# Reordering the start of the attention steps in the compressed-key layers of a four-layer hybrid transformer

## The chip, the cores and the metric

The kernel runs on one core of one Trainium2 chip. The metric is device time in microseconds of one execution, as a median over executions. Lower is better.

## The reference

Four layers over 512 tokens of width 1024 (16 heads of 64). Each layer is a mixer and a gated convolutional feed-forward part, with RMS norms around both. The mixers are, in order: nsa (compressed keys, selected keys, local window), stick-breaking, sliding window with sinks, and nsa again. The change concerns the two nsa layers. Cut to what matters:

```python
q, k_cmp, v_cmp, k_sel, v_sel, k_win, v_win, g_logit = split(h @ w_in)
ck, cv = compress(k_cmp, 0), compress(v_cmp, 1)        # 31 compressed keys for each of 4 groups
for each block i of 128 queries, each group g, each head r of the group:
    p_cmp = masked_softmax(q @ ck.T * scale - slope * dist_c);   o_cmp = p_cmp @ cv
    # the 16 best blocks of 64 keys are asked for, and there are only 8: all are selected
    p_s   = masked_softmax(q @ k_sel.T * scale - slope * dist);  o_sel = p_s @ v_sel
    p_w   = masked_softmax(q @ k_win.T * scale - slope * dist);  o_win = p_w @ v_win
    out   = g0 * o_cmp + g1 * o_sel + g2 * o_win
return out @ w_out
```

All is float32. masked_softmax divides by max(sum, 1e-30); that maximum is the "floor" below.

## The kernel before

**Weights and panels.** Weights stream from HBM in units of 128 x 1024 through a ring of four (L239). ScalarE rounds a unit to its high part (L260, `split_hi`), VectorE forms the low part (L266, `split_lo`), and TensorE multiplies high by high, low by high and high by low (L304 to L306, and L917 to L919 in key and value panels). A panel is four units into four of the eight PSUM banks. Panel S holds selected keys and values, panel W the window ("local") ones.

**Between the panels.** While TensorE works on S and W, VectorE makes the softmax of the compressed scores (`lowered`, `weighted`, `turned`, L1835 to L1851), takes the selected keys out of PSUM into the scratch `ktmp` (`dve_k`, L1002), and forms their low halves in `kl` (`dve_k_low`, L967 and L974), which raises `k_ready`. ScalarE copies values (`act_v`, L1007) and the keys' high halves (`act_k`, L957). `ktmp` lies at the address `u2_at`, and so does `qs`, the queries of the current group, split in two: ScalarE writes the high half (L1347), VectorE the low half (L1407), four of each for the four heads of a group. Since both share the address, the first queries wait for `k_ready`.

**Steps.** Behind the panels come 64 steps (`STEPS`): 4 groups x 2 kinds of keys (selected, then local) x 2 pairs of heads x 4 query blocks, the largest first (`step_of`: i = 3, 2, 1, 0, with i + 1 key blocks). For each step t and both heads of the pair:

1. TensorE `scores(t)` (L1285, L1286), issued four steps ahead. The first two (`ahead`) are issued inside W's last unit, the third behind it and behind `pe.wait_ge(evac_v, v_after[W + 1])`, the evacuation of the local keys.
2. VectorE `biased(t)` (L1419): bias and row minimum.
3. ScalarE `exps(t)` (L1355): exponential and sum.
4. VectorE `floor(t)` (L1450) and `inverse(t)` (L1455) of the sums.
5. GpSimd `weighted(t)` (L1501): times inverse and gate. It raises `nd_done`.
6. TensorE `transposes(t)` (L1298) into two PSUM banks.
7. ScalarE `copy(t)` of the first bank (L1363) and VectorE `copy(t)` of the second (L1429). For i = 3 and 2 each head has a bank. For i = 1 both heads lie in the first bank (ScalarE's), for i = 0 both lie in the second (VectorE's).
8. TensorE `values(t)` (L1319).

The order on each engine is written out by hand: `pe_steps`, `act_steps`, `dve_steps`, `pool_steps`. TensorE runs transposes(t), scores(t + 4), values(t - 1) in each step. VectorE's local keys are `window_keys` (L1002 again, into `kts`); their low halves (`window_low`, L1437 and L1440) are spread over steps 1 to 8. The output of two heads is `output` on ScalarE (L1374) and `low` on VectorE (L1445), the latter raising `o_ready`. Then follows the output projection (`pe_out`).

VectorE's order at the head of the steps:

```python
queries(0, 0)
queries(0, 1)
biased(0)
biased(1)
window_keys()
queries(0, 2)
queries(0, 3)
for t in range(2):
    floor(t)
    inverse(t)
biased(2)
biased(3)
```

Of the kernel before, what the change touches and what calls it, by code (L numbers as in the profile page):

```python
# [6 lines left out]
F32 = mybir.dt.float32  # L7
# [5 lines left out]
P = 128  # L13
D = 1024
T = 512
# [88 lines left out]
def hybrid_layers(nc, ins, out, kinds=KIND):  # L104
# [7 lines left out]
    with ExitStack() as ctx:  # L112
# [660 lines left out]
        for c, start in ((0, t_start), (1, o_at)):  # L773
            xcf.append(Space(start, start + 8 * K)(f"xcf{c}", [P, 16, G, N_CMP], F32))
            xcl.append(Space(start, start + 8 * K)(f"xcl{c}", [P, 16, G, N_CMP], F32R))
            xch.append(Space(start + 8 * K, start + 16 * K)(f"xch{c}", [P, 16, G, N_CMP], F32R))
        ktmp = Space(u2_at, u2_at + 4 * K)("ktmp", [P, 2, T], F32)
        hs = Space(o_at, o_at + 8 * K)
# [482 lines left out]
        def act_copies(t):  # L1261
            return 3 * (t // 4) + (1, 2, 3, 3)[t % 4]
# [4 lines left out]
        def pe_steps(pe, l, last_unit):  # L1267
# [20 lines left out]
            def transposes(t):  # L1288

                it, b, p, i = step_of(t)  # L1290
                pe.wait_ge(nd_done, 2 * (B + t) + 2)
                if t:
                    pe.wait_ge(nca_done, C3 + act_copies(t - 1))
                    pe.wait_ge(ncd_done, C3 + dve_copies(t - 1))
                for a in range(2):
                    x, at_ = turned_at(t, a)
                    for j in range(i + 1):
                        mm = nc.tensor.transpose(psum[:, half_of(l, 4 + x), at_ + j * P:at_ + (j + 1) * P],  # L1298
                                                 raw_scores(t, a)[:, j * P:(j + 1) * P], ident[:])
                    mm.then_inc(nt_done, 1)  # L1300
# [36 lines left out]
            values(STEPS - 1)  # L1337

        def act_steps(act, l, window_values):
            k = nsa_before[l]  # L1340
            B = STEPS * k

            def queries(it, r):
                s_ = slice(64 * (r % 2), 64 * (r % 2) + 64)
                if it:
                    act.wait_ge(nz_done, 2 * (B + 16 * (it - 1) + 8 + 4 * (r // 2) + 4))
                nc.scalar.activation(qs[s_, r, :], qt[s_, 2 * it + r // 2, :], ACT.Copy, scale=1.0 / slope(R * it + r)).then_inc(qh_done, 1)  # L1347

# [26 lines left out]

            act.wait_ge(k_ready, kr_before[l] + 2)
            for r in range(R):
                queries(0, r)
            exps(0)
# [3 lines left out]
            for t in range(STEPS):  # L1383
                it, x = t // 16, t % 16
                if step_of(t)[3]:
                    copy(t)
                if t + 3 < STEPS:
                    exps(t + 3)
                if it == 0 and x in (1, 3, 5, 7):
                    window_twin(x // 2)  # L1390
                if it + 1 < G and x in (8, 9, 12, 13):
                    queries(it + 1, (8, 9, 12, 13).index(x))
                if x == 13:
                    output(2 * it)
                if x == 1 and it:
                    output(2 * it - 1)
            output(DC - 1)

        def dve_steps(dve, ch, l, window_keys):
            k = nsa_before[l]  # L1400
            B = STEPS * k

            def queries(it, r):
                a = r % 2
                s_, d_ = slice(64 * a, 64 * a + 64), slice(64 * (1 - a), 64 * (1 - a) + 64)
                dve.wait_ge(qh_done, heads_before[l] + R * it + r + 1)
                nc.vector.scalar_tensor_tensor(qs[d_, r, :], qt[s_, 2 * it + r // 2, :], 1.0 / slope(R * it + r),  # L1407
                                               qs[s_, r, :].bitcast(F32), ALU.mult, ALU.subtract).then_inc(qs_ready, 1)

# [46 lines left out]

            mark = [0]
            queries(0, 0)
            queries(0, 1)
            biased(0)  # L1460
            biased(1)
            window_keys()
            queries(0, 2)
            queries(0, 3)
            for t in range(2):
                floor(t)
                inverse(t)
            biased(2)
            biased(3)
            for t in range(STEPS):  # L1470
                it, x = t // 16, t % 16
                if t + 2 < STEPS:
                    floor(t + 2)
                if step_of(t)[3] != 1:
                    copy(t)
                if t + 2 < STEPS:
                    inverse(t + 2)
                if t + 4 < STEPS:
                    biased(t + 4)
                if it == 0 and 1 <= x <= 8:  # L1480
                    window_low(x - 1)
                if it + 1 < G and x in (9, 10, 13, 14):
                    queries(it + 1, (9, 10, 13, 14).index(x))
                if x == 14:
                    low(2 * it)
                if x == 2 and it:
                    low(2 * it - 1)
# [217 lines left out]
        def act_nsa(act, ch, l):  # L1705
# [25 lines left out]
            def exps(half):  # L1731
                act.wait_ge(ca_done, 2 * k + half + 1)
                v = sp_[:, 2 * half:2 * half + 2, :]
                nc.scalar.activation(v, v, ACT.Exp, scale=-1.0).then_inc(ce_done, 1)

            exps(0)
            act_v(act, ch, 0, p0 + 4, u0 + 24)
# [7 lines left out]
        def dve_nsa(dve, ch, l):  # L1745
# [106 lines left out]

            lowered(0)
            dve_k(dve, ch, l, 0, p0 + 4, u0 + 24, 2)
            dve.wait_ge(kt_done, kc_before[l] + 2)
            dve.sem_inc(evac_v, 1)
            split_lo(dve, u0 + 24 + AHEAD)
            lowered(1)
# [552 lines left out]
```

## Time and profile before

| what | value |
|---|---|
| median of 3 runs | 2602.22 us (2601.59 to 2604.24) |
| the profiled execution | 2604.24 us |
| its span in the trace | 2602.5 us |
| mean granted TensorE clock | 0.994 |
| TensorE busy | 2525.7 us, 97% |
| VectorE / ScalarE / GpSimd busy | 62% / 45% / 18% |

The span runs from the first to the last instruction of the program. "Idle before" a group is the time its engine stood still just ahead of it, and the arrow names what released it. PEclk is the share of TensorE's full clock that was granted. Times in the trace are in us from the span's start. The first nsa layer's steps run from about 151 to 303, the fourth layer's from about 2023 to 2174.

### The profile page before, as it was taken

The page shows a single profiled execution, that of the slowest core. Times are in us where ns is not written, and L with a number is a line of the kernel's source. Part 1 is how long each engine was busy: PE and PEld are TensorE (multiplying, and loading weights), DVE is VectorE, ACT ScalarE, POOL GpSimd, SP SyncE. Part 2 cuts the span into 40 slices and gives each one's busy share as a digit, 9 for nine tenths or more (in the row PEclk, how much of TensorE's full clock was granted, in tenths as well). Part 3 has the DMA queues.
Part 4 walks back from the last instruction along what each step waited for, and adds up shares of the span by engine and source line. Part 5 has one row for each costly group of instructions (what it writes and reads, how often), then busy time and mean ns, then how long its engine had stood idle before and what let it go on. Part 6 is the DMA issues. An engine that isn't in the chain of part 4 may idle for free.

```text
span 2602.5 us, 38223 instructions
## 1 busy us (share of the span) xinstructions
PE 2525.7 (97%) x13336; PEld 2076.2 (80%) x13336; DVE 1623.6 (62%) x2773; ACT 1171.2 (45%) x2007; POOL 473.1 (18%) x514
## 2 busy tenths in 40 slices
PE   8999999999999999999999999999999899999997
PEld 6977778888878677888878878888879777788886
DVE  6588567664263847667256677663385884766733
ACT  4367554443232844444235554442343674544421
POOL 2035321110010612111010021110010452211100
PEclk9999999999999999999999999999999999999999
DMA  4410123333233022333321123333333001233231
GB/s 159 140 33 2 33 79 100 97 97 97 75 109 97 17 65 92 96 96 94 103 79 61 42 81 100 96 96 99 97 106 108 17 2 51 88 97 97 89 105 49
DMA packets 61909, 210.91 MB, mean 81 GB/s; under 512 B 8528, under 2 KB 10320, under 8 KB 61776
## 3 DMA queue, kind: packets, MB, share of 16 engines
q1 hardware_dynamic: 61776, 209.13, 25.6%
q8 instruction: 84, 1.38, 0.2%
q14 instruction: 49, 0.40, 0.0%
HBM read 207.01 MB, written 2.10 MB: 80 GB/s over the span
## 4 chain that ended last, share of the span: by engine, by line
PE 86%; DVE 10%; ACT 2%; issue 1%; POOL 1%; DMA 0%; DVEq 0%; SPq 0%; POOLq 0%; ACTq 0%
PE psum L304 21%; PE psum L306 21%; PE psum L305 21%; PE psum L1298 3%; PE psum L1319 2%; PE psum L917 2%; PE psum L918 2%; PE psum L919 2%; DVE xl L477 2%; DVE h L494 2%; PE psum L1286 1%; PE psum L1285 1%; PE psum L338 1%; DVE dh L493 1%; PE psum L332 1%
## 5 line engine op out<-in xcount | busy, mean ns | idle before, releaser
L304 PE MATMUL psum<-xh,w_hi 128*128 128x512 f32 x1712 | 666.7, 389 | 0.2 <-DVE w_lo L266 0.2
L305 PE MATMUL psum<-xh,w_lo 128*128 128x512 f32 x1712 | 666.1, 389 | 0.0
L306 PE MATMUL psum<-xl,w_hi 128*128 128x512 f32 x1712 | 666.1, 389 | 0.0
L266 DVE TENSOR_TENSOR w_lo<-w_raw,w_hi 128x1024 fp32r<-128x1024 f32 x226 | 279.9, 1250 | 531.4 <-ACT w_hi L260 529.3
L260 ACT ACTIVATE w_hi<-w_raw 128x1024 fp32r<-128x1024 f32 x226 | 236.0, 1057 | 591.7 <-PE psum L306 465.1
L306 PEld LDWEIGHTS psum<-xl,w_hi 128*128 128x128 f32 x1712 | 321.3, 188 | 66.9
L304 PEld LDWEIGHTS psum<-xh,w_hi 128*128 128x128 f32 x1712 | 321.3, 188 | 66.8 <-issue 0.6
L305 PEld LDWEIGHTS psum<-xh,w_lo 128*128 128x128 f32 x1712 | 321.4, 188 | 66.5
L698 DVE TENSOR_TENSOR w_lo<-w_raw,w_hi 128x1024 fp32r<-128x1024 f32 x160 | 209.3, 1308 | 253.8 <-ACT w_hi L694 253.8
L669 POOL TENSOR_TENSOR cv<-cv 128x512 f32<-128x512 f32 x88 | 133.9, 1521 | 792.9 <-ACT cv L623 785.4
L694 ACT ACTIVATE w_hi<-w_raw 128x1024 fp32r<-128x1024 f32 x160 | 168.4, 1053 | 234.8 <-PE psum L306 234.8
L305 PE MATMUL psum<-ah,w_lo 128*128 (+1 forms) x704 | 273.9, 389 | 0.0
L304 PE MATMUL psum<-ah,w_hi 128*128 (+1 forms) x704 | 273.9, 389 | 0.0
L306 PE MATMUL psum<-al,w_hi 128*128 (+1 forms) x704 | 273.9, 389 | 0.0
L618 ACT ACTIVATE cv<-xo,conv_b,conv_w 128x512 f32<-128x512 f32 x176 | 129.2, 805 | 95.4 <-DVE xo L642 95.4
L651 DVE SCALAR_TENSOR_TENSOR cv<-xo,conv_w,cv 128x512 f32<-128x512 f32 x176 | 169.6, 1003 | 0.6 <-DVE xo L642 0.6
L305 PEld LDWEIGHTS psum<-ah,w_lo 128*128 128x128 f32 x704 | 132.1, 188 | 27.5
L304 PEld LDWEIGHTS psum<-ah,w_hi 128*128 128x128 f32 x704 | 132.1, 188 | 27.5
L306 PEld LDWEIGHTS psum<-al,w_hi 128*128 128x128 f32 x704 | 132.1, 188 | 27.3
L623 ACT ACTIVATE cv<-cv 128x512 f32<-128x512 f32 x88 | 55.0, 625 | 173.6 <-DVE cv L656 173.6
L1501 POOL TENSOR_SCALAR scores<-scores,rsums,gat 128x384 f32<-128x384 f32 (+1 forms) x128 | 98.2, 777 | 190.0 <-DVE rsums L1455 190.0
L332 PE MATMUL psum<-xh,w_hi 128*128 128x512 f32 (+1 forms) x284 | 105.8, 379 | 23.5 <-ACT xh L553 12.9
(217 smaller groups left out, 4049.0 us busy)
## 6 DMA issues: line engine op xcount, KB each, us to landing
w_raw<-w_up SPq DMA_DIRECT2D x176, 512.0 KB, 3.6
w_raw<-w_down SPq DMA_DIRECT2D x88, 512.0 KB, 3.6
w_raw<-nsa_in SPq DMA_DIRECT2D x56, 512.0 KB, 4.1
w_raw<-sb_in SPq DMA_DIRECT2D x24, 512.0 KB, 3.6
w_raw<-nsa_out SPq DMA_DIRECT2D x16, 512.0 KB, 3.6
w_raw<-swa_in SPq DMA_DIRECT2D x10, 512.0 KB, 3.6
w_raw<-sb_out SPq DMA_DIRECT2D x8, 512.0 KB, 3.7
w_raw<-swa_out SPq DMA_DIRECT2D x8, 512.0 KB, 3.6
```

Of the source, the lines that this page charges most:

```text
L260: nc.scalar.activation(w_hi[:, u % RING, :], w_raw[:, u % RING, :], ACT.Copy).then_inc(hi_done, 1)
L266: nc.vector.tensor_tensor(w_lo[:, u % RING, :], w_raw[:, u % RING, :], w_hi[:, u % RING, :].bitcast(F32), ALU.subtract).then_inc(split_don ...
L304: nc.tensor.matmul(bank(p, o), wh[:, k, o, :], xhi(k), start=(first and k == 0), stop=False)
L305: nc.tensor.matmul(bank(p, o), wl[:, k, o, :], xhi(k), start=False, stop=False)
L306: mm = nc.tensor.matmul(bank(p, o), wh[:, k, o, :], xlo(k), start=False, stop=(last and k == 1))
L332: nc.tensor.matmul(bank(p, o)[:, lo:hi], wh[:, k, o, :], xh[:, c, lo:hi], start=(c == 0 and lo == 0), stop=False, skip_group_check=True)
L618: nc.scalar.activation(cv[:, o, :], xo[:, o, 2:T + 2], ACT.Identity, bias=conv_b[:, bass.ds(cc, 1)], scale=conv_w[:, 2, bass.ds(cc, 1)]).t ...
L651: marks.append(ch.then(nc.vector.scalar_tensor_tensor(cv[:, o, :], xo[:, o, 1:T + 1], conv_w[:, 1, bass.ds(cc, 1)], cv[:, o, :], ALU.mult, ...
L669: nc.gpsimd.tensor_tensor(cv[:, 2 + a, :], cv[:, a, :], cv[:, 2 + a, :], ALU.mult).then_inc(prod_done, 1)
L694: nc.scalar.activation(w_hi[:, u % RING, :], w_raw[:, u % RING, :], ACT.Copy).then_inc(hi_done, 1)
L698: nc.vector.tensor_tensor(w_lo[:, u % RING, :], w_raw[:, u % RING, :], w_hi[:, u % RING, :].bitcast(F32), ALU.subtract).then_inc(split_don ...
L1501: nc.gpsimd.tensor_scalar(v, v, rsums[:, c:c + 1], gat[:, i, x:x + 1], ALU.mult, ALU.mult).then_inc(nd_done, 1)
```

## The change

Five moves, all in the nsa layers:

- `ktmp` goes to the address `o_at`, so the queries' buffer is free earlier. The queries of group 0 are split ahead of the compressed exponentials on ScalarE, and around the evacuation of the selected keys on VectorE, two ahead and two behind. ScalarE's wait for `k_ready` ahead of them goes. The functions move out as `act_query` and `dve_query`.
- On VectorE the floors and inverses of steps 0 and 1 go ahead of the local keys.
- TensorE's transpositions wait for the bank that they write, ScalarE's or VectorE's, in place of both at the start of a step.
- VectorE's copy for i = 0 goes ahead of the floor.
- `low(2 * it)` goes from the 15th step of a group to the 16th.

```diff
@@ -774,7 +774,7 @@
             xcf.append(Space(start, start + 8 * K)(f"xcf{c}", [P, 16, G, N_CMP], F32))
             xcl.append(Space(start, start + 8 * K)(f"xcl{c}", [P, 16, G, N_CMP], F32R))
             xch.append(Space(start + 8 * K, start + 16 * K)(f"xch{c}", [P, 16, G, N_CMP], F32R))
-        ktmp = Space(u2_at, u2_at + 4 * K)("ktmp", [P, 2, T], F32)
+        ktmp = Space(o_at, o_at + 4 * K)("ktmp", [P, 2, T], F32)
         hs = Space(o_at, o_at + 8 * K)
         hb = hs("hb", [NX, 2, CMP_HID], F32)
         hid = hs("hid", [P, 2, NX], F32)
@@ -1289,11 +1289,12 @@
 
                 it, b, p, i = step_of(t)
                 pe.wait_ge(nd_done, 2 * (B + t) + 2)
-                if t:
-                    pe.wait_ge(nca_done, C3 + act_copies(t - 1))
-                    pe.wait_ge(ncd_done, C3 + dve_copies(t - 1))
                 for a in range(2):
                     x, at_ = turned_at(t, a)
+                    if t and x == 0:
+                        pe.wait_ge(nca_done, C3 + act_copies(t - 1))
+                    elif t:
+                        pe.wait_ge(ncd_done, C3 + dve_copies(t - 1))
                     for j in range(i + 1):
                         mm = nc.tensor.transpose(psum[:, half_of(l, 4 + x), at_ + j * P:at_ + (j + 1) * P],
                                                  raw_scores(t, a)[:, j * P:(j + 1) * P], ident[:])
@@ -1336,15 +1337,24 @@
                     values(t - 1)
             values(STEPS - 1)
 
+        def act_query(act, l, it, r):
+            s_ = slice(64 * (r % 2), 64 * (r % 2) + 64)
+            if it:
+                act.wait_ge(nz_done, 2 * (STEPS * nsa_before[l] + 16 * (it - 1) + 8 + 4 * (r // 2) + 4))
+            else:
+                act.wait_ge(q_done, qn_before[l] + 2)
+            nc.scalar.activation(qs[s_, r, :], qt[s_, 2 * it + r // 2, :], ACT.Copy, scale=1.0 / slope(R * it + r)).then_inc(qh_done, 1)
+
+        def dve_query(dve, l, it, r):
+            a = r % 2
+            s_, d_ = slice(64 * a, 64 * a + 64), slice(64 * (1 - a), 64 * (1 - a) + 64)
+            dve.wait_ge(qh_done, heads_before[l] + R * it + r + 1)
+            nc.vector.scalar_tensor_tensor(qs[d_, r, :], qt[s_, 2 * it + r // 2, :], 1.0 / slope(R * it + r),
+                                           qs[s_, r, :].bitcast(F32), ALU.mult, ALU.subtract).then_inc(qs_ready, 1)
+
         def act_steps(act, l, window_values):
             k = nsa_before[l]
             B = STEPS * k
-
-            def queries(it, r):
-                s_ = slice(64 * (r % 2), 64 * (r % 2) + 64)
-                if it:
-                    act.wait_ge(nz_done, 2 * (B + 16 * (it - 1) + 8 + 4 * (r // 2) + 4))
-                nc.scalar.activation(qs[s_, r, :], qt[s_, 2 * it + r // 2, :], ACT.Copy, scale=1.0 / slope(R * it + r)).then_inc(qh_done, 1)
 
             def exps(t):
                 n = (step_of(t)[3] + 1) * P
@@ -1373,9 +1383,6 @@
                 act.wait_ge(nv_done, B + 16 * (c // 2) + 12 + 4 * (c % 2))
                 nc.scalar.activation(xh[:, c, :], psum[:, half_of(l, 6 + c % 2), :], ACT.Copy).then_inc(oh_done, 1)
 
-            act.wait_ge(k_ready, kr_before[l] + 2)
-            for r in range(R):
-                queries(0, r)
             exps(0)
             exps(1)
             window_values()
@@ -1389,7 +1396,7 @@
                 if it == 0 and x in (1, 3, 5, 7):
                     window_twin(x // 2)
                 if it + 1 < G and x in (8, 9, 12, 13):
-                    queries(it + 1, (8, 9, 12, 13).index(x))
+                    act_query(act, l, it + 1, (8, 9, 12, 13).index(x))
                 if x == 13:
                     output(2 * it)
                 if x == 1 and it:
@@ -1399,13 +1406,6 @@
         def dve_steps(dve, ch, l, window_keys):
             k = nsa_before[l]
             B = STEPS * k
-
-            def queries(it, r):
-                a = r % 2
-                s_, d_ = slice(64 * a, 64 * a + 64), slice(64 * (1 - a), 64 * (1 - a) + 64)
-                dve.wait_ge(qh_done, heads_before[l] + R * it + r + 1)
-                nc.vector.scalar_tensor_tensor(qs[d_, r, :], qt[s_, 2 * it + r // 2, :], 1.0 / slope(R * it + r),
-                                               qs[s_, r, :].bitcast(F32), ALU.mult, ALU.subtract).then_inc(qs_ready, 1)
 
             def biased(t):
 
@@ -1455,23 +1455,22 @@
                 nc.vector.reciprocal(rsums[:, 16 + c:18 + c], rsums[:, 8 + c:10 + c]).then_inc(nw_done, 1)
 
             mark = [0]
-            queries(0, 0)
-            queries(0, 1)
             biased(0)
             biased(1)
-            window_keys()
-            queries(0, 2)
-            queries(0, 3)
             for t in range(2):
                 floor(t)
                 inverse(t)
+            window_keys()
             biased(2)
             biased(3)
             for t in range(STEPS):
                 it, x = t // 16, t % 16
+                i = step_of(t)[3]
+                if i == 0:
+                    copy(t)
                 if t + 2 < STEPS:
                     floor(t + 2)
-                if step_of(t)[3] != 1:
+                if i >= 2:
                     copy(t)
                 if t + 2 < STEPS:
                     inverse(t + 2)
@@ -1480,8 +1479,8 @@
                 if it == 0 and 1 <= x <= 8:
                     window_low(x - 1)
                 if it + 1 < G and x in (9, 10, 13, 14):
-                    queries(it + 1, (9, 10, 13, 14).index(x))
-                if x == 14:
+                    dve_query(dve, l, it + 1, (9, 10, 13, 14).index(x))
+                if x == 15:
                     low(2 * it)
                 if x == 2 and it:
                     low(2 * it - 1)
@@ -1733,6 +1732,8 @@
                 v = sp_[:, 2 * half:2 * half + 2, :]
                 nc.scalar.activation(v, v, ACT.Exp, scale=-1.0).then_inc(ce_done, 1)
 
+            for r in range(R):
+                act_query(act, l, 0, r)
             exps(0)
             act_v(act, ch, 0, p0 + 4, u0 + 24)
             split_hi(act, u0 + 24 + AHEAD)
@@ -1851,9 +1852,13 @@
                 nc.vector.tensor_copy(ct[:, :, i * P:(i + 1) * P], bank(p0 + 5, 2 + i % 2).rearrange("p (g q) -> p g q", q=P)).then_inc(cpt_ready, 1)
 
             lowered(0)
+            dve_query(dve, l, 0, 0)
+            dve_query(dve, l, 0, 1)
             dve_k(dve, ch, l, 0, p0 + 4, u0 + 24, 2)
             dve.wait_ge(kt_done, kc_before[l] + 2)
             dve.sem_inc(evac_v, 1)
+            dve_query(dve, l, 0, 2)
+            dve_query(dve, l, 0, 3)
             split_lo(dve, u0 + 24 + AHEAD)
             lowered(1)
             weighted(0)
```

## Rows read from the trace of the kernel before

**Rows 1.** The page, part 1: busy time, share and instructions of each engine.

```profile
PE 2525.7 (97%) x13336; PEld 2076.2 (80%) x13336; DVE 1623.6 (62%) x2773; ACT 1171.2 (45%) x2007; POOL 473.1 (18%) x514
```

**Rows 2.** TensorE's waits, 120 to 320: us in total, times, longest.

```profile
PE psum L1298 <- DVE pt L1429: 3.9, 7, 1.2
PE psum L1285 <- DVE qs L1407: 2.6, 1, 2.6
PE psum L1298 <- POOL scores L1501: 2.4, 1, 2.4
```

**Rows 3.** TensorE's waits over the whole span.

```profile
PE psum L332 <- ACT xh L553: 12.9, 7, 1.9
...
PE psum L1298 <- DVE pt L1429: 8.1, 15, 1.2
```

**Rows 4.** Timeline of TensorE: start, us, instruction, idle before it, releaser.

```profile
154.07 0.47 PE L1285 MATMUL psum<-kh,qs 128*128 128x512 f32 x1 [2.63 <-DVE qs L1407]
...
160.34 0.38 PE L1285 MATMUL psum<-kh,qs 128*128 128x256 f32 x1
...
163.86 1.09 PE L1298 MATMUL psum<-ident,scores 128*128 128x128 f32 x8 [2.39 <-POOL scores L1501]
```

**Rows 5.** Windows: length, busy time of each engine, PEclk, DMA share, GB/s.

```profile
155.10:158.40 3.30, 3.30 (x10) 2.89 (x9) 2.06 (x8) 2.72 (x8) 0.00 (x0) 0.50 0.08 31
165.30:168.60 3.30, 3.30 (x13) 2.96 (x12) 2.79 (x10) 2.24 (x8) 2.34 (x5) 0.50 0.03 7
...
1882.20:1885.50 3.30, 3.30 (x14) 2.91 (x13) 3.23 (x6) 2.68 (x4) 0.00 (x0) 0.50 0.91 291
```

**Rows 6.** Timeline of VectorE, 126 to 161.

```profile
126.44 1.29 DVE L1002 TENSOR_TENSOR ktmp<-psum,rb 128x512 f32<-128x512 f32 x2 [1.86 <-PE psum L919]
129.34 1.23 DVE L266 TENSOR_TENSOR w_lo<-w_raw,w_hi 128x1024 fp32r<-128x1024 f32 x1 [1.62 <-ACT w_hi L260]
...
150.38 0.86 DVE L974 CAST kl<-kl 64x512 fp32r<-64x512 f32 x2
...
154.81 0.69 DVE L1419 CUSTOM_DVE_ANT_0 scores<-psum,dist 128x512 f32<-128x512 f32 x1 [0.89 <-PE psum L1286]
...
157.13 0.08 DVE L1419 DVE_READ_ACCUMULATOR2_ANT mins<- 128x1 f32 x1
158.94 1.29 DVE L1002 TENSOR_TENSOR kts<-psum,rb 128x512 f32<-128x512 f32 x2 [1.72 <-PE psum L919]
160.38 1.40 DVE L1407 SCALAR_TENSOR_TENSOR qs<-qt,qs 64x512 fp32r<-64x512 f32 x2 [0.15 <-DVE kts L1002]
```

**Rows 7.** Timeline of ScalarE, 119 to 165.

```profile
124.62 1.06 ACT L1734 ACTIVATE scores<-scores 128x1024 f32<-128x1024 f32 x1 [6.28 <-DVE scores L1838]
...
151.26 2.59 ACT L1347 ACTIVATE qs<-qt 64x512 fp32r<-64x512 f32 x4 [1.49 <-DVE kl L974]
155.54 0.72 ACT L1355 ACTIVATE scores<-scores,mins 128x512 f32<-128x512 f32 x1 [1.69 <-DVE mins L1419]
...
158.07 0.19 ACT L1355 ACTIVATION_READ_ACCUMULATOR scores<-scores,mins 128x1 f32 x1
```

**Rows 8.** The chain that ended last, at GpSimd's first products.

```profile
162.29 0.22 POOL scores L1501
...
163.04 0.78 POOL scores L1501
```

**Rows 9.** Timeline of all engines, 189.5 to 192.5: step 12.

```profile
189.90 1.99 POOL L1501 TENSOR_SCALAR scores<-scores,rsums,gat 128x512 f32<-128x512 f32 x2 [1.18 <-DVE rsums L1455]
...
191.28 0.64 DVE L1450 TENSOR_SCALAR rsums<-rsums 128x2 f32<-128x2 f32 x1
...
192.38 0.30 PE L1298 MATMUL psum<-ident,scores 128*128 128x128 f32 x1 [1.18 <-DVE pt L1429]
```

**Rows 10.** Windows of groups 0 and 1, from first transposition to first transposition.

```profile
163.86:201.00 37.14, 35.25 (x305) 27.90 (x305) 33.12 (x118) 29.46 (x85) 24.29 (x36) 0.95 0.01 2
201.00:236.00 35.00, 34.14 (x309) 26.66 (x310) 28.58 (x117) 27.65 (x83) 20.13 (x33) 1.00 0.01 1
```

## The prediction, made before the changed kernel was run

> **What bounds the kernel now.** I read the page first. TensorE is busy for 97% of the span, VectorE for 62%, ScalarE for 45%, GpSimd for 18% [rows 1]. A change that only reorders work can therefore give back only what TensorE stands idle, or what it runs at a low clock. Next I read TensorE's waits for the first compressed-key (nsa) layer alone [rows 2]. Three kinds fall into it: 2.6 us once, for the low halves of the queries (L1407), 2.4 us once, for GpSimd's weighted probabilities (L1501), and 3.9 us in seven pieces, for VectorE's copies of transposed probabilities (L1429). The fourth layer is the same code, and the whole-span row for L1429 has 8.1 us in 15 pieces [rows 3]. I work out one layer and double it.
>
> The timelines show where the two long stalls stand. The first scores begin at 154.07 after 2.63 us, the first transposition at 163.86 after 2.39 us [rows 4]. Each is followed by a stretch at granted clock 0.50 (the 1.2 GHz level): 155.1 to 158.4, and 165.3 to 168.6 [rows 5]. So a stall is paid once as idle time and a second time in half-speed matmuls. Scores and the rest of the panel took 160.34 - 154.07 = 6.27 us [rows 4]. At full rate I estimate 4.7 us: four products of 512 at 0.23, four of 384 at 0.17, half a unit at 1.38 + 1.6, taken from the starts in the stretch at full clock. The cost is 1.6 us. For the second stretch I take 1.5 us, the 3.3 us at half speed less a little waiting inside it.
>
> **The change, part by part, from 151.44 on, in one layer.**
>
> *Queries early.* The scratch of the selected keys leaves the queries' address, so the eight splits can run before the keys are done. On ScalarE four cost 2.59 us and go into a wait of 6.28 us [rows 7]. On VectorE two cost 1.40 us (0.69 each, L1407 at 160.38) and go into the wait of 1.86 us ahead of the keys at 126.44; the other two come behind the keys (1.29 us, to 127.7) and end at 129.1, and the next instruction began at 129.34 [rows 6]. All of it is covered; uncovered it would be 2.8 us on VectorE. The first scores then wait for the lows of the selected keys, whose last cast ends at 150.38 + 0.86 = 151.24 [rows 6]. That is 0.2 us ahead of TensorE's need at 151.44, so they start at 151.4. Gain 2.6 us, and 1.6 us of half clock: the first unit ends at 151.4 + 4.7 = 156.1 in place of 160.34. No DMA is moved; the weights' high halves stand ahead of ScalarE's queries in its order, as before.
>
> *Floors and inverses ahead of the local keys.* VectorE still has a weight split first, to 152.4. The four biased scores took 157.13 + 0.08 - 154.81 = 2.40 us, so they end at 154.8 [rows 6]. ScalarE's exponentials end 3.45 us behind the first biased one (154.81 to 158.26) [rows 6, 7]: 155.85. The second floor needs these, so floors and inverses end at 156.35. Only then come the local keys, 1.29 us [rows 6]: 157.65. In front of its third scores TensorE waits for just that evacuation. It was ready at 156.1 and goes on at 157.75: a new stall of 1.65 us. Two scores of 256 and two of 128 columns take 1.0 us, and transposition 0 starts at 158.8. GpSimd needed 163.82 - 162.29 = 1.53 us for its first two products [rows 8]; they now begin at 155.3, and hide. So 163.86 becomes 158.8: 5.06 us gained (2.6 + 1.6 + 2.4 - 1.65 = 4.95 by parts, the same within rounding). What is queued behind the floors is the evacuation, and all of TensorE waits for it.
>
> Without a long stall the second half-clock stretch goes too: 1.5 us.
>
> *Transposition waits by bank, and the one-block copy ahead of the floor.* Beyond the two stalls I count 4.1 us of small ones in this layer: 3.9 us [rows 2] and 0.2 us of pieces under 0.16 us. At step 12 TensorE waits 1.18 us. VectorE's floor lasts 0.64 us there, where its others take 0.17, and ends at 191.92, just as GpSimd's pair does (189.90 + 1.99 = 191.89); the copy comes behind it [rows 9]. Putting the copy first takes it out from behind the floor, but transposition 12 also needs GpSimd's pair, so only 192.38 - 192.0 = 0.4 us comes back. The other six waits make 3.9 - 1.2 = 2.7 us [rows 2], 0.36 to 0.51 us each. Five stand at steps 16, 28, 32, 44 and 48, where GpSimd's pair ends some 0.1 us ahead of TensorE, so I take all of them: 2.2 us. The sixth, 0.5 us at step 61, is for a copy of three blocks; with waits by bank its first three transpositions go ahead, and 0.35 us comes back. Sum 3.0 us, between 0 and 4.1.
>
> *The low half of the output one step later.* It costs the same 0.69 us and now follows the copy. Its reader in the next group comes two steps later, at about 238, and it ends near 236.3. Nothing.
>
> *What is late next.* In the first group VectorE also splits the local keys. It is busy 33.12 us there, against 28.58 in the next group [rows 10], and its timeline shows no wait from 173 to 193. Group 0 took 37.14 us and would now take about 34.8, so VectorE has hardly any room. Some of what TensorE gains at the beginning comes back at step 12, since VectorE's idle 2.2 us before 173.2 existed only because TensorE was slow. I charge 0.7 us, between 0 and 1.5 us.
>
> Sum for one layer: 2.6 + 1.6 + 2.4 - 1.65 + 1.5 + 3.0 - 0.7 = 8.75 us; for two, 17.5 us. The profiled execution has a span of 2602.5 us within its own 2604.24; the median of the three is 2602.22. 2602.5 - 17.5 = 2585.0 for the span, and 2602.2 - 17.5 = 2584.7 for the time.
>
> **A rule to weigh.** The floor that ends with GpSimd's pair [rows 9] is a row about a shared path. The Trainium skill (SBUF - State Buffer, section "Who interferes with whom") says that a VectorE instruction in a two-port mode and a GpSimd instruction exclude each other for the whole of whichever began first. It speaks against this change in one place: the second floor now comes while GpSimd works on its first products. By the rule it waits up to one product, 0.7 us, and the evacuation and TensorE behind it with it; the sum would be 2584.9 to 2586.1, against 2584.7 with a floor of 0.17 us.
>
> **The rivals.**
>
> *The new stall brings the half clock back.* TensorE has seven idle times of 12.9 / 7 = 1.84 us in the span [rows 3]; behind two of them the clock fell to 0.50, at 1882.2 and at 2223.5, and not behind the other five (the first of the two is in [rows 5]). Behind all four of 2.4 to 2.6 us it fell, behind the two of 1.18 us it did not. A stall of 1.65 us lies below, so a fall is perhaps one in four for each layer, at 1.6 us: 2586.3 with one, 2587.9 with two.
>
> *VectorE becomes the bound of the steps.* If it runs late through all groups, the 3.0 us of small waits stay and the charge doubles: 2 x 3.7 us less, 2592.1. For it speaks the busy time of group 0; against it the 6.4 us that VectorE stands idle in group 1, of 35.0 [rows 10].
>
> *Everything gives way.* No new stall, all small waits gone, no charge: 2 x 3.45 us more, 2577.8. Against it: the evacuation stands behind the second floor in one queue.
>
> *The queries do not let the scores go.* If the four splits delay VectorE's softmax, the lows of the keys come late by the same, and 2.6 + 1.6 us fall away in each layer: 2593.1. The covers above speak against it.
>
> *Slower than before.* The floors wait for ScalarE, and the evacuation of the local keys waits behind them. If that chain were late for another reason, TensorE would stand at this one wait. It would have to stand 1.65 + 8.75 = 10.4 us in each layer before the change loses. The exponentials are four instructions of about 0.7 us, so nothing in the profile makes that so long.
>
> **How the numbers follow.** Forecast, no clock fall or one of them, with its own range 2582 to 2588: 0.58. Two falls, or VectorE somewhat later than charged: 0.12. VectorE the bound: 0.13. Everything gives way: 0.10. Queries without effect: 0.04. Slower: 0.03. The prediction is 2585.0, the worked-out 2584.7 rounded toward the cases above it. The range reaches from 2579 (nearly all gives way) to 2593 (small waits unmended, or both falls with some lateness), and leaves about one in ten on the whole outside. 0.2%, about what a measurement of this kernel can tell from no change, is 5.2 us. All cases but the last lie below 2597; for gains that shrink further than any of these I keep 0.04. Faster 0.93, within 0.2% 0.04, slower 0.03.
>
> **What would show it.** First scores some 0.1 us behind the panel's matmul in place of 2.63. A wait of TensorE for L1002 of 1 to 2 us ahead of the third scores, which is not there now. No wait for L1501 at the first transposition. Both L1347 and L1407 near 118 to 129. Small waits on L1429 under 2 us in a layer. The clock at 1.00 through 151 to 175. The prediction is wrong if the first scores still wait, if the stall at the local keys is over 3 us, or if VectorE shows no idle time in groups 1 to 3 while TensorE waits for it.

## The result, and the profile after

The changed kernel takes 2586.23 us (median of 4 runs, 2583.41 to 2587.39), against 2603.23 us for the kernel before in the same comparison. The ratio is 0.9933, with a 95% interval of 0.9918 to 0.9948. The prediction was 2585.0 in a range of 2579 to 2593. The profiled execution took 2587.39 us, with a span of 2585.6.

The page's first part, to be read against [rows 1]: TensorE is busy 3.7 us less though it does the same matmuls, and the span is 16.9 us shorter, so 13.2 us of idle time went and the rest is clock.

```profile
span 2585.6 us, 38223 instructions
...
PE 2522.0 (98%) x13336; PEld 2073.5 (80%) x13336; DVE 1623.5 (63%) x2773; ACT 1170.1 (45%) x2007; POOL 472.6 (18%) x514
```

TensorE's waits over the whole span (us in total, times, longest). The copies (L1429), 8.1 us in [rows 3], are gone, and so are the queries (2.6 us in each layer, [rows 2]). In their place stands L1285, released by VectorE's queue, 1.6 us in each layer. GpSimd's products (now L1500) hold 1.8 us where they held 4.8. The line with 4.8 is of the kernel before, the others of the changed one:

```profile
PE psum L1298 <- POOL scores L1501: 4.8, 2, 2.4
```

```profile
PE psum L332 <- ACT xh L553: 13.0, 7, 1.9
...
PE psum L1285 <- DVEq L1878: 3.2, 2, 1.6
PE psum L1299 <- POOL scores L1500: 1.8, 2, 1.0
```

TensorE's timeline in the first layer, against [rows 4]. The first scores follow the panel without a wait, the third ones wait 1.61 us, and the first transposition follows at once. The last line is step 12, against [rows 9].

```profile
151.68 0.47 PE L1285 MATMUL psum<-kh,qs 128*128 128x512 f32 x1
...
157.94 0.39 PE L1285 MATMUL psum<-kh,qs 128*128 128x256 f32 x1 [1.61 <-DVEq L1878]
...
158.93 1.85 PE L1299 MATMUL psum<-ident,scores 128*128 128x128 f32 x8
...
187.01 1.09 PE L1299 MATMUL psum<-ident,scores 128*128 128x128 f32 x8 [0.97 <-POOL scores L1500]
```

VectorE's timeline, against [rows 6]. The four early splits (L1352) take what was idle; the weight split behind them starts at 129.69, at once behind its high half (ScalarE's, 128.60 + 1.06 = 129.66). The second floor waits 0.83 us for ScalarE's exponentials, and the local keys (`kts`) come only behind it:

```profile
124.96 1.41 DVE L1352 SCALAR_TENSOR_TENSOR qs<-qt,qs 64x512 fp32r<-64x512 f32 x2
126.79 1.29 DVE L1002 TENSOR_TENSOR ktmp<-psum,rb 128x512 f32<-128x512 f32 x2 [0.42 <-PE psum L919]
128.23 1.40 DVE L1352 SCALAR_TENSOR_TENSOR qs<-qt,qs 64x512 fp32r<-64x512 f32 x2 [0.15 <-DVE ktmp L1002]
129.69 1.23 DVE L266 TENSOR_TENSOR w_lo<-w_raw,w_hi 128x1024 fp32r<-128x1024 f32 x1
...
155.24 0.17 DVE L1455 RECIPROCAL rsums<-rsums 128x2 f32<-128x2 f32 x1
156.23 0.22 DVE L1450 TENSOR_SCALAR rsums<-rsums 128x2 f32<-128x2 f32 x1 [0.83 <-ACT scores L1365]
156.48 0.17 DVE L1455 RECIPROCAL rsums<-rsums 128x2 f32<-128x2 f32 x1
156.56 1.27 DVE L1002 TENSOR_TENSOR kts<-psum,rb 128x512 f32<-128x512 f32 x2
```

Windows of the changed kernel, columns as in [rows 5]. TensorE is busy 1.79 of the 3.4 us around the new stall, and the 3.3 us behind it run at granted clock 0.50:

```profile
155.50:158.90 3.40, 1.79 (x16) 1.59 (x15) 1.98 (x7) 2.27 (x8) 3.33 (x5) 1.00 0.08 34
159.10:162.40 3.30, 3.30 (x13) 2.81 (x12) 2.22 (x11) 2.22 (x9) 0.65 (x2) 0.50 0.03 7
```

Groups 0 and 1, against [rows 10]. Group 0 has 0.97 us of idle time left and group 1 none, at 34.01 us where it took 35.00:

```profile
158.93:195.08 36.15, 35.18 (x306) 27.78 (x305) 33.38 (x121) 29.92 (x86) 22.13 (x34) 0.95 0.01 2
195.08:229.09 34.01, 34.01 (x310) 26.61 (x309) 28.48 (x115) 27.50 (x83) 20.10 (x32) 1.00 0.01 1
```

For all kernels below I measure the same stretches in the trace of each: from the end of the panel's matmul ahead of the first scores to the first transposition ("start"), the four groups of steps, and the sum to the first matmul of the output projection ("layer"). "Low" counts the half-clock stretches inside it. Values are us in the first layer; the value in brackets is the fourth layer's.

| kernel | start | group 0 | group 1 | group 3 | layer | low, 1st (4th) | span |
|---|---|---|---|---|---|---|---|
| before | 12.42 | 37.14 | 34.96 | 32.47 | 151.94 (152.10) | 2 (2) | 2602.5 |
| changed | 7.15 | 36.16 | 34.01 | 32.11 | 143.42 (143.22) | 1 (1) | 2585.6 |
| e1 queries only | 6.67 | 35.51 | 34.95 | 32.47 | 144.57 (144.56) | 0 (0) | 2588.0 |
| e2 keys first | 6.66 | 34.67 | 34.01 | 32.12 | 141.45 (141.43) | 0 (0) | 2582.0 |
| e3 steps only | 12.41 | 35.96 | 34.01 | 32.11 | 148.50 (148.42) | 2 (2) | 2595.2 |
| e4 wait moved, one floor | 5.29 | 35.29 | 34.01 | 32.11 | 140.71 (140.72) | 0 (0) | 2580.2 |
| e5 no bank waits | 7.14 | 36.58 | 34.04 | 32.52 | 144.32 (143.81) | 1 (1) | 2587.1 |
| e6 bank waits only | 12.40 | 34.47 | 34.06 | 32.16 | 147.13 (147.05) | 1 (1) | 2592.9 |
| e7 lows spread | 7.14 | 33.45 | 34.13 | 32.11 | 140.83 (140.86) | 0 (0) | 2579.8 |
| e8 wait moved | 6.25 | 34.71 | 34.02 | 32.11 | 141.10 (141.40) | 0 (0) | 2581.8 |
| e9 changed again | 7.13 | 34.66 | 34.01 | 32.11 | 141.92 (141.92) | 0 (0) | 2582.4 |
| e10 keys first again | 6.66 | 34.67 | 34.01 | 32.11 | 141.45 (141.53) | 0 (0) | 2580.5 |
| e11 combined | 5.30 | 34.89 | 34.14 | 32.11 | 140.48 (140.45) | 0 (0) | 2579.3 |
| e12 combined, old copy | 5.30 | 34.43 | 34.14 | 32.11 | 140.00 (140.04) | 0 (0) | 2579.1 |

The two layers together lost 17.4 us (304.04 to 286.64), against 16.9 for the span; the rest of the program is the same within 0.6 us. Over all kernels the rest lies between 2297.6 and 2299.3 us. Nearly all of that is the time ahead of the steps: the panel's matmul ahead of the first scores ends between 150.5 (e10) and 152.3 (e12). So differences of a microsecond are read from the layers, not from spans or times. The changed kernel and e1 to e12 were timed in four sets, the last three on different chips; the kernel before took 2603.23 us in the first, 2602.41 in that of e1 to e4, 2602.88 (one execution) in that of e5 to e8 and 2602.48 in that of e9 to e12.

### The profile page after: what moved, and what is told of

Same layout as the page of the kernel before. It is cut to its first block, busy times and chain, and to the rows that moved or that the text cites. A ratio compares the mean times of both kernels' runs of the same rounds, so it can differ in the third digit from the quotient of the medians.

```text
span 2585.6 us, 38223 instructions
## 1 busy us (share of the span) xinstructions
PE 2522.0 (98%) x13336; PEld 2073.5 (80%) x13336; DVE 1623.5 (63%) x2773; ACT 1170.1 (45%) x2007; POOL 472.6 (18%) x514
## 4 chain that ended last, share of the span: by engine, by line
PE 88%; DVE 9%; ACT 1%; issue 1%; POOL 1%; DMA 0%; DVEq 0%; SPq 0%; POOLq 0%; ACTq 0%
PE psum L304 21%; PE psum L306 21%; PE psum L305 21%; PE psum L1299 3%; PE psum L1320 3%; PE psum L917 2%; PE psum L919 2%; PE psum L918 2%; DVE xl L477 2%; DVE h L494 2%; PE psum L1286 1%; PE psum L1285 1%; PE psum L338 1%; DVE dh L493 1%; PE psum L332 1%
## 5 line engine op out<-in xcount | busy, mean ns | idle before, releaser
L1500 POOL TENSOR_SCALAR scores<-scores,rsums,gat 128x384 f32<-128x384 f32 (+1 forms) x128 | 98.1, 776 | 170.1 <-DVE rsums L1455 170.1
```

What stands on the lines that cost most here:

```text
L1500: nc.gpsimd.tensor_scalar(v, v, rsums[:, c:c + 1], gat[:, i, x:x + 1], ALU.mult, ALU.mult).then_inc(nd_done, 1)
```

## The experiments

**e1: the early queries alone**, on the kernel before.

```diff
-        ktmp = Space(u2_at, u2_at + 4 * K)("ktmp", [P, 2, T], F32)
+        ktmp = Space(o_at, o_at + 4 * K)("ktmp", [P, 2, T], F32)
...
+            for r in range(R):
+                act_query(act, l, 0, r)
             exps(0)
             act_v(act, ch, 0, p0 + 4, u0 + 24)
```

> The kernel before with the early queries alone (scratch moved, splits moved); local keys ahead of the floors as before, waits and copies as before. My theory: the first scores start at once and the local keys are evacuated while TensorE still works on its unit, so there is no wait at the third scores. The floors then come behind the keys, and the first transposition waits about 1.1 us for GpSimd's products: first transposition 6.7 us behind the first scores, where the changed kernel has 7.2. The small waits of 4.1 us in a layer stay. Span 2 x (2.6 + 1.6 + 1.3 + 0.5) = 12 us below before, 2590.5; up to 3 us more if the shorter stall no longer brings a half-clock stretch. Rival: without the floors ahead the first transposition waits its old 2.4 us, and the span is 2594 or more.

Measured: 2589.23 us (median of 4 runs), ratio 0.9947 (0.9932 to 0.9962), span 2588.0. The first transposition stood 6.78 us behind the first scores. TensorE's waits in the first layer, by L1298: the two long ones of [rows 2] are one of 1.0 us, and the small ones are just as they were.

```profile
PE psum L1298 <- DVE pt L1428: 3.9, 7, 1.2
PE psum L1298 <- POOL scores L1496: 1.0, 1, 1.0
```

What follows: the early queries give 7.4 and 7.5 us a layer by themselves, the larger part of the change, and do not need the floors ahead. 3.2 us of it is clock, two stretches of 1.6. No half-clock stretch was left, which makes 14.5 us of span in place of the 12 I had summed up, as the expectation allowed.

**e2: the local keys ahead of the floors again**, on the changed kernel.

```diff
+            window_keys()
             for t in range(2):
                 floor(t)
                 inverse(t)
-            window_keys()
```

> The changed kernel with the local keys ahead of the two floors again; all else stays. My theory: the wait of 1.61 us at the third scores goes and one of about 1.1 us comes at the first transposition, so each layer is 0.5 us shorter in idle time, and if a stall of 1.1 us brings no half-clock stretch, 1.5 us more: span between 2581.5 and 2584.6 against 2585.6. Rival, that the floors ahead are what the change needs: the first transposition waits 2.4 us as before, and the span is 2587 or more.

Measured: 2583.73 us (median of 4), ratio 0.9926 (0.9911 to 0.9941), span 2582.0. TensorE's timeline: the third scores run at once, and the first transposition waits 0.95 us.

```profile
156.77 0.39 PE L1285 MATMUL psum<-kh,qs 128*128 128x256 f32 x1
...
158.86 1.09 PE L1299 MATMUL psum<-ident,scores 128*128 128x128 f32 x8 [0.95 <-POOL scores L1500]
```

What follows: with the queries early, the floors ahead of the keys lose. The start is 6.66 us without them and 7.15 with them. The rest of the difference is clock and is taken up at e9.

**e3: the three moves inside the steps alone**, on the kernel before: waits by bank, the one-block copy ahead of the floor, `low` at the 16th step.

> The kernel before with the three moves inside the steps alone: waits by bank, one-block copy ahead of the floor, low half one step later. My theory: both long stalls of 2.6 and 2.4 us and both half-clock stretches stay; of the small waits of 4.1 us in a layer some 0.8 us at step 12 are left. Span 6.0 to 6.8 us below before, about 2596. Rival, VectorE as the bound of the steps: less than 2 us below.

Measured: 2594.94 us (median of 6), ratio 0.9971 (0.9959 to 0.9983), span 2595.2. The start is as long as before and both half-clock stretches stayed; a layer is 3.4 to 3.7 us shorter, and the wait at step 12 is 0.81 and 0.86 us. The gain of 7.5 us is a little over the 6.0 to 6.8 that I expected. VectorE is not the bound.

**e4: the evacuation wait at the first transposition, and one floor ahead of the keys**, on the changed kernel.

```diff
                 window(3, begin)
-                pe.wait_ge(evac_v, v_after[W + 1])
...
                 pe.wait_ge(nd_done, 2 * (B + t) + 2)
+                if t == 0:
+                    pe.wait_ge(evac_v, v_after[plan.mix_p[l] + 7])
...
-            for t in range(2):
-                floor(t)
-                inverse(t)
+            floor(0)
+            inverse(0)
             window_keys()
+            floor(1)
+            inverse(1)
```

> The changed kernel with two more moves: TensorE's wait for the evacuation of the local keys goes from the third scores to the first transposition (scores 2 and 3 write other banks), and of the two floors only the first stands ahead of the local keys. My theory: no wait at the third scores; GpSimd's first pair and the evacuation are both done within 0.1 us of the end of scores 3, so no idle time over 0.3 us and no half-clock stretch up to step 12. Span 2 x (1.6 + 1.5) = 6.2 us below the changed kernel, about 2579.5. Rival, that the half clock does not hang on this stall: it falls anyway, and the span is 2582.5.

Measured: 2581.89 us (median of 5), ratio 0.9919 (0.9906 to 0.9933), span 2580.2. The start fell to 5.29 us with no wait in it, and no half-clock stretch came. But step 1 now waits, which I had not foreseen, and step 12 kept 0.8 us:

```profile
PE psum L1301 <- POOL scores L1503: 0.8, 1, 0.8
PE psum L1301 <- ACT pt L1375: 0.6, 1, 0.6
```

**e5: the old wait for both copies**, on the changed kernel.

```diff
+                if t:
+                    pe.wait_ge(nca_done, C3 + act_copies(t - 1))
+                    pe.wait_ge(ncd_done, C3 + dve_copies(t - 1))
                 for a in range(2):
                     x, at_ = turned_at(t, a)
-                    if t and x == 0:
-                        pe.wait_ge(nca_done, C3 + act_copies(t - 1))
-                    elif t:
-                        pe.wait_ge(ncd_done, C3 + dve_copies(t - 1))
```

> The changed kernel with TensorE's old wait for both copies at the start of a transposition step; the copy order and the later low half stay. If each small wait has its own remover (my theory), the waits at steps 16, 28, 32, 44 and 48 stay gone, since the copy and the low half were moved, group 1 still takes 34.0 us, and only 0.35 us comes back at step 61: span 0.7 us longer for this part. Rival, that the waits by bank carry the gain: group 1 goes back toward 34.9 us, and each layer is some 3 us longer.

Measured: one execution, 2588.84 us, span 2587.1. Group 1 takes 34.04 us. The waits on copies are at step 61 (0.51) and, in group 0, 0.24 and 0.36 at steps 5 and 9; the last two I had not expected. The span is 1.5 us longer than the changed kernel's, where I expected 0.7:

```profile
PE psum L1298 <- DVE pt L1428: 1.1, 3, 0.5
PE psum L1298 <- POOL scores L1499: 0.7, 1, 0.7
```

**e6: the waits by bank alone**, on the kernel before (the diff of e5 turned round).

> The kernel before with the waits by bank alone. Transpositions 16, 28, 32, 44, 48 then start on ScalarE's bank while VectorE's copy of the other still runs: four of them take 0.42 us and cover a wait of 0.36 to 0.51. If the two ways are substitutes, group 1 takes 34.0 to 34.15 us here too and a layer is 2.7 to 3.3 us shorter than before with both long stalls kept; step 12 keeps about 0.8 us. If each wait has its own remover, group 1 stays at 34.9 and a layer gains 0.35 us alone.

Measured: one execution, 2594.73 us, span 2592.9. All waits of the transpositions (now L1299) on copies are gone; step 12 keeps 0.92 us, for GpSimd. Group 1 in its window has no idle time:

```profile
PE psum L1299 <- POOL scores L1502: 3.3, 2, 2.4
PE psum L1285 <- DVE qs L1408: 2.6, 1, 2.6
```

```profile
164.20:167.60 3.40, 3.40 (x23) 3.15 (x24) 2.84 (x9) 2.43 (x9) 3.10 (x6) 1.00 0.03 7
...
198.63:232.69 34.06, 34.06 (x311) 26.59 (x309) 28.46 (x117) 27.52 (x83) 20.12 (x32) 1.00 0.01 1
```

What follows from both: the two ways are substitutes. Either the waits by bank or the moved copy and low half take group 1 from 34.96 to 34.05 us; together they give no more. The waits by bank also mend step 61, and steps 5 and 9, which wait in e5 and not in e6. The moved copy and the later low half were not run apart from each other. The first line shows that the wait of 2.4 us at the first transposition is followed by full clock here. A half-clock stretch in group 0 costs 1.6 us (35.51 us in e1, with none, against 37.14), so a layer is 4.8 us shorter: 3.2 by the waits and 1.6 by the clock.

**e7: low halves of the local keys spread**, on the changed kernel.

```diff
-                if it == 0 and 1 <= x <= 8:
+                if it == 0 and 1 <= x <= 4:
                     window_low(x - 1)
+                if it == 1 and 1 <= x <= 4:
+                    window_low(x + 3)
```

> The changed kernel with the low halves of the local keys of groups 2 and 3 formed in steps 1 to 4 of group 1 in place of steps 5 to 8 of group 0: 2.2 us of VectorE's work leaves group 0 and goes where VectorE stands idle. If VectorE's load in group 0 makes step 12 late (my theory), the wait of 0.97 and 0.80 us there is gone, group 1 stays at 34.0 us, and a layer is 0.8 to 1.0 us shorter. Rival, that GpSimd's pair of 2.0 us is late by its own slowness: the wait stays at 0.8 or more.

Measured: one execution, 2581.56 us, span 2579.8. The wait at step 12 is gone in both layers. GpSimd's pair still takes 2.00 us; it only starts in time. TensorE has one wait left in the layer, and group 1, which took on the work, costs 0.12 us more. Against e9 below, the changed kernel at full clock, a layer is 1.1 us shorter (141.92 to 140.83):

```profile
PE psum L1285 <- DVEq L1880: 1.6, 1, 1.6
```

```profile
158.20:161.60 3.40, 3.40 (x24) 3.05 (x24) 3.01 (x15) 3.40 (x13) 1.24 (x3) 1.00 0.02 7
158.13:191.58 33.45, 33.45 (x307) 26.42 (x306) 29.83 (x117) 29.80 (x86) 21.66 (x34) 1.00 0.01 2
```

The first of these lines is the stretch behind the stall of 1.6 us, and its clock is 1.00. The same stall was followed by 0.50 in the changed kernel's profile.

**e8: the evacuation wait moved alone** (e4 with both floors ahead).

> The changed kernel, both floors ahead of the local keys, with TensorE's wait for the evacuation moved from the third scores to the first transposition alone. My theory: scores 2 and 3 run at once, and the wait of 1.61 us shrinks by their 1.0 us to 0.7 at the first transposition; each layer 0.9 us shorter. After a stall of 0.7 us no half-clock stretch, so span 1.8 to 5 us below the changed kernel's 2585.6. Rival: the half clock falls here as well, and the gain is 1.8 us at most.

Measured: one execution, 2583.61 us, span 2581.8. The start is 0.90 us shorter, with a stall of 0.79 us (0.81 in the fourth layer) and no half-clock stretch. Against e9, at full clock too, a layer is 0.8 and 0.5 us shorter.

**e9: the changed kernel once more.**

> The changed kernel once more, as the mark for the next one. Its start holds a stall of 1.6 us in each layer; if whether the half clock follows is a matter of where the stall happens to fall, the profile of this run shows it after neither, one or both (1.5 us each), and its times spread over about 3 us: 2583.4 to 2587.4, as before.

Measured: 2584.2 us (median of 5, 2583.64 to 2585.97), ratio 0.9931 (0.9918 to 0.9945). The profile has the stall (1.60 us) in both layers, and no half clock behind either. Windows behind the stall in the first and the fourth layer:

```profile
157.80:161.20 3.40, 3.40 (x27) 3.14 (x27) 2.46 (x12) 2.39 (x11) 1.22 (x3) 1.00 0.00 0
...
2019.20:2022.60 3.40, 3.37 (x26) 3.10 (x27) 2.43 (x12) 2.39 (x11) 1.22 (x3) 1.00 0.01 2
```

**e10: keys first once more**, on the same chip as e9.

> Keys ahead of floors again, on the same chip as the changed kernel. My theory (the floors ahead are a loss): 2 to 3.5 us faster than the changed kernel, with less spread since its stall of 0.95 us is not followed by a half-clock stretch: 2583 to 2584. Rival: the difference seen so far was between chips, and the two come out within 1 us of each other.

Measured: 2583.22 us (median of 5, 2582.34 to 2583.66), ratio 0.9925 (0.9912 to 0.9939). It is 1.0 us below e9, where I expected 2 to 3.5; that is the number of the rival. The two intervals overlap, so the times alone do not tell the two apart. The traces do: at full clock in both, a layer takes 141.45 (141.53) and 141.92 us, 0.47 and 0.39 less, 0.9 for both. So the order itself is worth 0.9 us. The 2.5 us between e2 and the changed kernel's first median hold something else besides: half-clock stretches, which its profile has, are the likely part.

**e11: combined**, e4 and e7 and one move more.

```diff
             window_values()
+            copy(0)
             exps(2)
             for t in range(STEPS):
                 it, x = t // 16, t % 16
-                if step_of(t)[3]:
+                if t and step_of(t)[3]:
                     copy(t)
```

> The changed kernel with the evacuation wait moved to the first transposition, one floor ahead of the local keys, the low halves of groups 2 and 3 in group 1, and ScalarE's first copy ahead of the exponentials of step 2. First transposition 5.3 us behind the panel's end, group 0 33.6 us, no stall over 0.3 us in the steps: 139.2 us a layer against 140.7 without the last two. Span 2577, time 2579, 23 us below before. Rival: the copy moved ahead makes the exponentials of step 2 late, and the third transposition waits instead: 2580 to 2582.

Measured: 2581.16 us (median of 5), ratio 0.9918 (0.9904 to 0.9931), span 2579.3. The rival was right in its number and its cause, though the wait is at the second transposition and not the third: in the place of the old 0.62 us came one of 1.00 us, at step 1. The layer took 140.48 us, where I expected 139.2. ScalarE's line, then VectorE's, then TensorE's. The exponentials of step 2 begin at 158.20; VectorE's floor of step 2 waits for them for 1.41 us, with its copy of step 0 behind it in the queue, and TensorE waits for that copy:

```profile
158.20 0.50 ACT L1367 ACTIVATE sp<-sp,mins 128x256 f32<-128x256 f32 x1
```

```profile
159.31 0.17 DVE L1453 TENSOR_SCALAR rsums<-rsums 128x2 f32<-128x2 f32 x1 [1.41 <-ACT sp L1367]
159.39 0.68 DVE L1432 COPY pt<-psum 128x512 f32<-128x512 f32 x1
```

```profile
160.13 0.55 PE L1301 MATMUL psum<-ident,scores 128*128 128x128 f32 x3 [1.00 <-DVE pt L1432]
```

**e12: the same without that last move.**

> The same with ScalarE's first copy in its old place. If that copy, behind the values and the exponentials of step 2, is what held step 1 by 0.62 us, this wait is here and not in the combined kernel, and group 0 takes 0.6 us longer.

Measured: one execution, 2580.93 us, span 2579.1. The wait at step 1 is 0.62 us, as in e4, and a layer is 0.4 to 0.5 us shorter than in e11, where I had expected it 0.6 us longer. It is the shortest layer of all, 140.00 us. Of the versions with a median over several executions e11 is the fastest, 3.0 us below the changed kernel on the same chip (2581.16 against 2584.2). The two intervals overlap, but all five executions of e11 (up to 2582.25) lie below all five of e9 (from 2583.64), and the traces agree (140.5 against 141.9 us a layer).

## Why the prediction was right

**Queries early.** Predicted 2.6 us, measured 2.73 (2.63 to no gap at all). The covers on both engines held: VectorE's weight split began at 129.69 where it had begun at 129.34, in a stage that stood 0.35 us later as a whole. The first unit took 4.65 us besides the new stall, predicted 4.7 (the terms listed for it add up to 4.58). e1 shows this part alone.

**Floors ahead of the keys.** The new stall was predicted at 1.65 us and is 1.61 in both layers, at the place and from the queue that the text named. The first transposition was to move from 12.42 us behind the panel to 7.36; it stands at 7.15. What I did not say is that this order is worse than the old one once the queries are early: e2 and e10 are 0.47 us a layer shorter with the keys first. All numbers for it were there (the keys could be evacuated while ScalarE still worked on its exponentials), but I only compared with the kernel before.

**The half clock.** The forecast had none behind the new stall, and gave one in four for it in each layer. Its sign of a clock at 1.00 from 151 to 175 did not come: the profile has a stretch behind both stalls. The two cost 1.5 and 1.3 us net (group 0 takes 36.16 and 35.94 us there, 34.66 in e9), 1.6 us each without the shorter wait at step 12 that came with them (0.97 and 0.80 us against 1.12). Over the profiles of kernels with this stall, it came in 4 of 8 cases: both layers of the changed kernel and of e5, neither in e7 and e9. So one in two is nearer than one in four, though on thin evidence: in each of the four profiles both layers went the same way. The same program had both stretches in one profile and none in the other, so whether they come is chance as far as this record goes. That the medians of 2586.2 and 2584.2 differ by it is argued, since only the profiled execution of each has a trace.

**Small waits.** I took 3.0 us less a charge of 0.7, so 2.3. e1 and e2 differ by just these three moves, at full clock and with the same start: 144.57 - 141.45 = 3.1 us. The mis-sized term is the charge. VectorE was late, as predicted: step 12 kept 0.97 and 0.80 us, and 1.12 in e9, where the text had 0.8 plus 0.7. But that is 0.3 us at most, nothing else suffered, and the small pieces and all of the 0.5 us at step 61 went too. VectorE also had more room than I saw: from 173 to 193 its timeline has three waits, 0.36, 0.16 and 0.35 us, where I read none. (The copy that step 61 waited for has four blocks, not three; the sum does not use it.) e7 confirms the cause: with 2.2 us of VectorE's work out of group 0 the wait goes, at the same 2.00 us of GpSimd.

**What removes them.** I credited the moved copy and low half with steps 16 to 48, and the waits by bank with step 61 alone. The amounts were right, the attribution was incomplete: e6 mends all of them with the waits by bank and nothing else, e5 mends the first five without them.

**The sum.** 8.75 us for a layer was made with the charge and no half clock. Measured are 8.5 and 8.9 us with the half clock (the changed kernel) and 10.0 and 10.2 without it (e9). So the closeness of 2585.0 to the measured span of 2585.6 owes something to luck, errors that cancel. In each layer I had about 1.3 us too little: 0.8 of small waits, 0.3 at the start (12.42 - 7.13 = 5.29 against the 4.95 of the parts), 0.1 in the second stretch at half clock. And I had not counted the new stretches, which took 1.5 and 1.3 us back.

**The rule weighed.** The Trainium skill (SBUF - State Buffer, "Who interferes with whom") has a VectorE instruction in a two-port mode and a GpSimd instruction exclude each other until the first has ended. I put the floor between GpSimd's products at 0.1 to 0.7 us by it. The second floor in the changed kernel took 0.22 us against 0.17, so it cost 0.05 here: it began at 156.23, and the first product ended at 156.28. In e4 the second floor took 0.30 us and ended at 156.90, with GpSimd's first pair at 156.87; the trace agrees with the rule on who waits, and the price was small because the product was nearly done. No row names the mode that the floor ran in.

## What to carry to other kernels

Compare a reordering with its own parts, not with the old kernel alone: this change gains 17 us and still holds a move that loses 0.9 (e10 against e9). When a stall goes, look which instruction now stands, in the order written for its engine, behind one that waits for a slower engine's result; here it was an evacuation behind two tiny instructions, and in e11 a copy behind a floor. Two cures for one wait may be substitutes, and only running each alone shows it. And where a clock stretch comes by chance, compare the stages of traces with the same clock, not two medians.

## What the runs showed of the hardware

All of this is one core's. A stall of 1.6 us in a stream of matmuls was followed by a half-clock stretch in 4 of 8 cases, with the same code around it. Stalls of 0.6 to 1.2 us in the nsa layers were never followed by one, those of 2.63 us always (6 of 6), and those of 2.4 us in 4 of 6: in e6 it stayed at full clock. Each such stretch cost about 1.6 us.

The seven stalls of 1.85 us elsewhere in the program ([rows 3]) were followed by one in 24 of 98 cases over the 14 profiles, one to three times in each. How many there are does not show in the end: from the end of the first layer's steps to the end of the fourth layer's panels the trace takes 1719.5 us with one of them (e9), 1719.5 with two (e2) and 1719.7 with three (e11), and 1719.4 to 1719.7 in all kernels. In e10 the matmuls behind the first of these stalls are 1.0 us late at first, and at the next stall, 366.9 us on, they are level with those of e9. What makes it up was not looked for.

The changed kernel's four executions spread over 4 us (2583.4 to 2587.4), while those of e2, without the long stall, spread over 1 us (2582.9 to 2583.8). Two stretches, at 1.6 us each, would account for most of that. This is argued from the profiles; the other executions have no trace, and the time ahead of the steps, which varies by 1.8 us over the profiles, has a part in it too.

GpSimd's pair of 512 columns takes 1.51 to 1.53 us at the first step and 1.99 to 2.00 at steps 12, 16, 28, 32, 44 and 48, with the next queries' splits on VectorE beside it. Step 60 has the same place in the last group, with no queries left to split, and takes 1.52. Steps 12 and 60 in the changed kernel, and the split beside the former:

```profile
184.96 2.00 POOL L1500 TENSOR_SCALAR scores<-scores,rsums,gat 128x512 f32<-128x512 f32 x2 [1.18 <-DVE rsums L1455]
286.26 1.52 POOL L1500 TENSOR_SCALAR scores<-scores,rsums,gat 128x512 f32<-128x512 f32 x2 [0.47 <-DVE rsums L1455]
```

```profile
185.62 0.69 DVE L1352 SCALAR_TENSOR_TENSOR qs<-qt,qs 64x512 fp32r<-64x512 f32 x1
```

This points at the splits; no run took them out alone.
